# The last norms of a fused two-block model: GpSimd subtracts some means, PSUM operands, and the final norm in two token halves

## The reference

```python
xl = _layernorm(ALPHA * xl + g * out, ln_g, ln_b)       # end of the first block
# second block
h = x * (1.0 + scale) + shift
proj = h @ w_in                                          # q, k, v, g_attn, glu_a, glu_b, g_conv
# ... banded attention; conv of glu_a * sigmoid(glu_b), 31 taps; pointwise product
y = concat([y_attn, y_conv]) @ w_out
x = layer_norm(ALPHA * x + gate * y, ln_g, ln_b)         # mean and variance over the 2048 features
```

## Time and profile before

| what | us |
|---|---|
| median of three runs | 3348.26 (3348.14 to 3349.41) |
| the profiled execution | 3346.11 |
| its span in the profile | 3344.4 |
| PE busy | 3196.6 (96%) |
| DVE busy | 2244.8 (67%) |
| ACT busy | 1324.6 (40%) |
| POOL busy | 265.5 (8%) |

### The profile page before, as it was taken

The page is one execution under the profiler, slowest core; times in us unless marked ns, Lnnn a source line. Parts: engine busy times, 40 slices in busy tenths (PEclk is TensorE's granted clock), DMA queues, the critical chain, the costliest instruction groups (busy, mean ns, idle before and its releaser), DMA issues.

```text
span 3344.4 us, 47678 instructions
## 1 busy us (share of the span) xinstructions
PE 3196.6 (96%) x16612; PEld 2606.6 (78%) x16612; DVE 2244.8 (67%) x3528; ACT 1324.6 (40%) x2023; POOL 265.5 (8%) x490
## 2 busy tenths in 40 slices
PE   5899999999999999999999999999997999999996
PEld 0799989788777777879888777777785877888885
DVE  0677778756777765687656676774677899755446
ACT  0445555323444443237422444443326222455323
POOL 0000011101101100110101000100110000000000
PEclk8899999999999999999999999999998999999998
DMA  9665557555444433654755444432562322222332
GB/s 397 253 226 200 205 191 269 189 214 186 143 153 165 147 114 122 241 192 170 262 187 202 160 139 147 156 116 74 210 215 104 114 101 88 95 90 80 113 114 88
DMA packets 107409, 554.41 MB, mean 166 GB/s; under 512 B 17856, under 2 KB 17904, under 8 KB 64144
## 3 DMA queue, kind: packets, MB, share of 16 engines
q1 hardware_dynamic: 47232, 343.95, 28.8%
q0 software_dynamic: 60048, 208.75, 18.4%
HBM read 530.55 MB, written 22.04 MB: 165 GB/s over the span
## 4 chain that ended last, share of the span: by engine, by line
PE 71%; DVE 9%; DVEq 6%; DMA 5%; issue 5%; ACT 2%; ACTq 1%; POOL 0%; POOLq 0%; SPq 0%
PE acc L1164 21%; PE acc L1166 20%; PE acc L1165 20%; DVEq L2213 4%; DVE w_lo L1589 3%; PE pv L1288 3%; DMA xy<-in_wm 3%; PE S L1262 2%; DMA gates<-in_wm 2%; PE S L1277 1%; DVE gates L1642 1%; DVE xy L2220 1%; PE misc L1299 1%; ACT w_hi L641 1%; DVE xy L2040 1%
## 5 line engine op out<-in xcount | busy, mean ns | idle before, releaser
L1164 PE MATMUL acc<-h_hi,w_hi 128*128 128x512 f32 (+1 forms) x4576 | 1672.5, 365 | 25.4 <-DVE w_lo L1589 14.9
L1166 PE MATMUL acc<-h_hi,w_lo 128*128 128x512 f32 (+1 forms) x4576 | 1641.5, 359 | 0.0
L1165 PE MATMUL acc<-h_lo,w_hi 128*128 128x512 f32 (+1 forms) x4576 | 1640.2, 358 | 0.0
L1164 PEld LDWEIGHTS acc<-h_hi,w_hi 128*128 128x128 f32 x4576 | 865.3, 189 | 182.4 <-issue 37.2
L1165 PEld LDWEIGHTS acc<-h_lo,w_hi 128*128 128x128 f32 x4576 | 866.2, 189 | 128.6 <-issue 6.9
L1166 PEld LDWEIGHTS acc<-h_hi,w_lo 128*128 128x128 f32 x4576 | 865.4, 189 | 129.6
L1589 DVE TENSOR_TENSOR w_lo<-raw,w_hi 128x1024 fp32r<-128x1024 f32 x592 | 698.1, 1220 | 200.7 <-ACT w_hi L641 197.7
L641 ACT ACTIVATE w_hi<-raw 128x1024 fp32r<-128x1024 f32 x592 | 592.9, 1052 | 65.3 <-DMA raw<-in_w 38.5
L641 ACT ACTIVATE ev<-acc 128x512 f32<-128x512 f32 (+1 forms) x210 | 110.7, 531 | 879.0 <-PE acc L1166 857.8
L465 POOL DMA_DIRECT2D gates<-in_wm x288 | 153.6, 533 | 1429.2 <-DVE gates L1642 1237.4
L641 ACT ACTIVATE work<-S,small 128x768 f32<-128x768 f32 (+1 forms) x160 | 129.1, 813 | 257.3 <-DVE small L1756 257.3
(11 more groups left out here) (244 smaller groups left out, 2425.8 us busy)
## 6 DMA issues: line engine op xcount, KB each, us to landing
raw<-in_w SPq DMA_DIRECT2D x296, 1024.0 KB, 4.9
gates<-in_wm POOLq DMA_DIRECT2D x288, 512.0 KB, 4.8
xy<-in_wm SPq DMA_DIRECT2D x32, 1024.0 KB, 8.8
x_d<-xy POOLq DMA_DIRECT2D x2, 4096.0 KB, 14.2
qb<-x_d POOLq DMA_DIRECT2D x16, 256.0 KB, 4.3
kb<-x_d POOLq DMA_DIRECT2D x16, 256.0 KB, 4.2
out_y<-xy POOLq DMA_DIRECT2D x4, 1024.0 KB, 4.2
bias_d<-kb POOLq DMA_DIRECT2D x8, 384.0 KB, 20.7
```

The lines of the kernel that those rows point to most:

```text
L1164: mm(o, w_hi[:, w], h_hi[:, x], start=n == 0, stop=False)
L1165: mm(o, w_hi[:, w], h_lo[:, x], start=False, stop=False)
L1166: last = mm(o, w_lo[:, w], h_hi[:, x], start=False, stop=n == len(ks) - 1)
```

## The change

Four things are changed.

1. Norm "b", statistics. The mean is written to `t1` once, and ACT squares it (`mean_sq`) in place of DVE. Tiles 0 to 3 are lowered by DVE straight from the PSUM sums; tiles 4 to 15 are lowered by POOL (12 `tensor_tensor` of 128x512), ahead of its store in its program. The inverse deviation is written to PSUM (`pv`), and ACT's plain copy of h goes to PSUM (`whole_glu`, two quarters of `S`). The split of the second `glu` weight tile is cut in halves: the first half comes before the last `bout` tile is taken out, DVE's second half after the third pair.
2. `glu` on ACT: each of the three groups of `norm_affine` moves from before the evacuation of tile 0, 1, 2 to behind it.
3. `out2`: the last two weight tiles (14 and 15) run as four products of 256 columns: both tiles for tokens 0 to 255, then both for 256 to 511. The statistics of the first token half are summed on PE inside the third of these; the whole last norm runs once for each token half. Of each half DVE lowers tiles 0 to 7 from PSUM and POOL tiles 8 to 15; DVE multiplies all 16. ACT applies gain and bias to tiles 0 to 10 of the first half and 0 to 11 of the second, POOL to 11 to 15 of the first, DVE to 12 to 15 of the second.
4. The output goes out in six stores from SP: two of the first half (8 tiles each), four of the second (8, 4, 2 and 2 tiles).

```diff
+        whole_glu = (S[:, 2 * SEQ:3 * SEQ], S[:, 3 * SEQ:4 * SEQ])
+        TOKENS = (slice(0, SEQ // 2), slice(SEQ // 2, SEQ))
+        POOL_FIRST, DVE_LAST = 11, 12
+        last_dev = (pv[:, 0:SEQ // 2], misc[:, 0:SEQ // 2])
...
@@ pool @@
             residual("b", "bout", x1_d)
+            pool.wait_ge(rest_ready, shown(rest_ready, 1))
+            for k in range(4, KT):
+                x = tile(xy, k, SEQ)
+                nc.gpsimd.tensor_tensor(x, x, t1[:], ALU.subtract).then_inc(rest_done, 1)
             store("b", x2_d, 48)
...
-            for q in range(4):
-                pool.wait_ge(x_ready, shown(x_ready, 48 + 4 * (q + 1)))
-                pool.dma_start(out[:, 4 * q:4 * (q + 1)], xy3[:, 4 * q:4 * (q + 1)]).then_inc(x_st, 16)
-            pool.wait_ge(x_st, shown(x_st, 48 + 64))
+            for h in range(2):
+                pool.wait_ge(last_rest_ready, shown(last_rest_ready, h + 1))
+                for k in range(8, KT):
+                    x = tile(xy, k, SEQ)[:, TOKENS[h]]
+                    nc.gpsimd.tensor_tensor(x, x, t1[:, TOKENS[h]], ALU.subtract).then_inc(last_rest_done, 1)
+                if h == 0:
+                    for k in range(POOL_FIRST, KT):
+                        ...
+                        nc.gpsimd.tensor_scalar(x, x, vec("ln_g2", k), vec("ln_b2", k), ALU.mult, ALU.add)\
+                            .then_inc(pool_out, 1)
@@ scalar @@
                 if c == "b":
-                    hi(At(TILE0["glu"] + 1))
-                    inverse_deviation("b")
+                    hi(At(TILE0["glu"] + 1), (1,))
+                    act.wait_ge(rest_ready, shown(rest_ready, 1))
+                    f(t2[:], t1[:], ACT.Square).then_inc(mean_sq, 1)
+                    inverse_deviation("b", pv)
...
             def glu(i, first=False):
...
-                    if first and p < 3:
-                        norm_affine("b", SEQ, 1, (0, 6, 11)[p], (6, 11, KT)[p])
                     (the wait for the tile and its evacuation)
+                    if first and p < 3:
+                        norm_affine("b", SEQ, 1, (0, 6, 11)[p], (6, 11, KT)[p])
...
+            for m in range(2):
+                new_square(0, m)
+            last_inverse(0)
+            new_square(1, 0)
+            last_affine(0, 0, POOL_FIRST)
+            new_square(1, 1)
+            last_inverse(1)
+            last_affine(1, 0, DVE_LAST)
@@ tensor @@
+            def last_tiles():
+                for h in range(2):
+                    for m in range(2):
+                        j, a = j_at("out2", 3, 2 + m), a_at("out2", 3, 2 + m)
+                        ... (h == 0: wait for acc_free; h == 1: wait for part_out)
+                        product(acc[a.odd][:, TOKENS[h]], j, range(KT), at=h * SEQ // 2, stride=SEQ, beside_n=6,
+                                beside=(lambda: last_deviation_sums(0)) if (h, m) == (1, 0) else None)\
+                            .then_inc(part_done, 1)
+                last_deviation_sums(1)
@@ vector @@
+                    def variance(h):
+                        cols = TOKENS[h]
+                        dve.wait_ge(stat_done, shown(stat_done, 2 * ST_NO[c] + 2 * h + 1))
+                        ts(t1[:, cols], last_sums[h][0], 1.0 / D, None, ALU.mult)
+                        dve.drain()
+                        dve.sem_inc(last_rest_ready, 1)
+                        ... (square of the mean; variance; then_inc(dev_ready, 1))
+                        for k in range(8):
+                            x = part(c, k)[:, cols]
+                            stt(x, last_sums[h][0], -1.0 / D, x, ALU.mult, ALU.add)
...
+                    evacuated(0, 0)
+                    evacuated(0, 1)
+                    squares(0)
+                    variance(0)
+                    evacuated(1, 0)
+                    scaled_part(0, 0, KT)
+                    evacuated(1, 1)
+                    squares(1)
+                    variance(1)
+                    scaled_part(1, 0, KT)
+                    dve.drain()
+                    for k in range(DVE_LAST, KT):
+                        x = part(c, k)[:, TOKENS[1]]
+                        ts(x, x, vec("ln_g2", k), vec("ln_b2", k), ALU.mult, ALU.add).then_inc(dve_out, 1)
...
-            scaled(0, 2)
-            def next_pair(i, more=True):
-                scaled(i * 2, 2)
-                modulated("g.h", SEQ, i - 1)
-                if more:
-                    less_rest(i * 2 + 2, 2)
-                    dve.drain()
-            loop(dve, 1, KT // 2 - 1, next_pair)
+            scaled(0, 2, pv)
+            def next_pair(i):
+                dve.wait_ge(rest_done, shown(rest_done, At(-2, 2, i)))
+                scaled(i * 2, 2, pv)
+                modulated("g.h", SEQ, i - 1, whole_glu)
+            loop(dve, 1, 4, next_pair)
+            lo(At(TILE0["glu"] + 1), (1,))
+            loop(dve, 4, KT // 2, next_pair)
```

More of the change, by code:

```diff
@@ L451, in _ @@
                 at += i * t
+            x_at = 48
+            for h, first, last, done, n in ((0, 0, 8, x_ready, x_at + 8), (0, 8, KT, pool_out, KT - POOL_FIRST),
+                                            (1, 0, 8, x_ready, x_at + POOL_FIRST + 8),
+                                            (1, 8, DVE_LAST, x_ready, x_at + POOL_FIRST + DVE_LAST),
+                                            (1, DVE_LAST, 14, dve_out, 14 - DVE_LAST),
+                                            (1, 14, KT, dve_out, KT - DVE_LAST)):
+                sp.wait_ge(done, shown(done, n))
+                if done is pool_out:
+                    sp.wait_ge(x_ready, shown(x_ready, x_at + POOL_FIRST))
+                sp.dma_start(out[:, first:last, TOKENS[h]], xy3[:, first:last, TOKENS[h]]).then_inc(out_st, 16)
+            sp.wait_ge(out_st, shown(out_st, 6 * 16))
         @block.gpsimd
@@ L871, in body, with deviation_squares @@
                             modulate_pair("a.h", early_x, SEQ, *by_set(0), n, to=whole_early)
[L873 to L875 removed]
+                def deviation_squares(i, tiles=range(4)):
+                    for p in tiles:
                         j, a, k = j_at(phase, i, p), a_at(phase, i, p), 4 * (i - 2) + p
@@ L907, in inverse_deviation @@
                 act.drain()
-                f(t2[:], t2[:], ACT.Exp, scale=-0.5).then_inc(ln_sd, 1)
+                f(to[:], t2[:], ACT.Exp, scale=-0.5).then_inc(ln_sd, 1)
             def squares_to_add(c, T, g, base=0):
@@ L1143, in _, with new_square, last_inverse, last_affine @@
             project_out("g", "out2", 4)
-            inverse_deviation("g")
-            norm_affine("g", SEQ, 2)
+            hi(At(TILE0["out2"] + KT - 1))
+            for k in (6, 7):
+                act.wait_ge(old_ready, shown(old_ready, 8 * ST_NO["g"] + k + 1))
+                act.wait_ge(ssq_added, shown(ssq_added, 16 * ST_NO["g"] + k + 3))
+                f(ev[(k + 6) % 4][:], tile(xy, k, SEQ), ACT.Square).then_inc(ssq_ready, 1)
+            def new_square(h, m):
+                n = 14 + 2 * h + m
+                act.wait_ge(part_out, shown(part_out, 2 * h + m + 1))
+                act.wait_ge(ssq_added, shown(ssq_added, 16 * ST_NO["g"] + n - 3))
+                f(ev[n % 4][:, TOKENS[h]], tile(xy, 14 + m, SEQ)[:, TOKENS[h]], ACT.Square).then_inc(ssq_ready, 1)
+            def last_inverse(h):
+                act.wait_ge(dev_ready, shown(dev_ready, ST_NO["g"] + h + 1))
+                f(t2[:, TOKENS[h]], t2[:, TOKENS[h]], ACT.Ln, bias=eps[:, 0:1])
+                act.drain()
+                f(last_dev[h], t2[:, TOKENS[h]], ACT.Exp, scale=-0.5).then_inc(ln_sd, 1)
+            def last_affine(h, first, last):
+                for k in range(first, last):
+                    x = tile(xy, k, SEQ)[:, TOKENS[h]]
+                    act.wait_ge(n_ready, shown(n_ready, LN_AT["g"] + KT * h + k + 1))
+                    f(x, x, ACT.Identity, scale=vec("ln_g2", k), bias=vec("ln_b2", k)).then_inc(x_ready, 1)
+            for m in range(2):
[6 more added lines that the diff above has]
+            last_affine(1, 0, DVE_LAST)
         @block.tensor
@@ L1391, in project_out, with body @@
                 T = TOK.get(c, SEQ)
-                def body(i, beside=None, beside_n=3, last=False):
-                    for p in range(4):
+                def body(i, beside=None, beside_n=3, last=False, tiles=range(4)):
+                    for p in tiles:
                         weight_tile(j_at(phase, i, p), a_at(phase, i, p), T, H_AT[c + ".y"], p == 0,
```

124 lines of the change are left out of this document (97 added, 27 removed).

## The result

The changed kernel takes 3332.52 us (median of five runs, 3330.49 to 3333.6); the kernel before, timed with it, 3349.39 (3348.14 to 3352.89). The ratio is 0.9949, 95% interval 0.9938 to 0.996: faster by 0.5%, inside the range, 0.7 us from the predicted 3333.2. The profiled execution took 3333.60 us, with a span of 3332.0.

The account below looks back on a forecast made before the run. PE holds 71% of the span, but glu is paced by DVE, whose run begins when x2's store lands. Gains of 5.1 us at the gated units' start and 10 at the end, 15.1 from 3348.26, give 3333.2 us; range 3325 to 3342.5.

Parts of the forecast that it names:

- A1: Norm b's statistics: first multiplication near 2534.6 instead of 2535.71, gain 1.1 us, from 0 to 1.6.
- A2: Pair loop: period falls from 4.16 to 2.82 us, paced by ACT; first pair of weight tiles ends 8.9 us earlier.
- PSUM operands: Pair loop operands moved to PSUM: no difference taken; 0.06 x 4 us on each pair hidden under ACT.
- The contention: DVE and POOL blocking one another over SBUF inputs: under 2 us added, as most DVE operations have one PSUM input.
- GpSimd: POOL's 12 subtractions in norm b: between 0.62 and 2.35 us each, estimate 1.1, hidden up to about 1.9 each.
- A3: Affines behind evacuations: x2's store leaves 16.1 us after the first pair, lands 5.1 us earlier; new PE wait 5 to 6.
- Part A: Norm b and the start of the gated units: gain 5.1 us, from 0 to 9, kept through glu by DVE.
- B: The kernel's end, out2's last tiles, last norm and stores: gain 9.7, say 10 us, from 4 to 13.
- (1): x2's store lands much sooner, 3 us more, and the DMA tail is 2 us shorter: 20 us, 3328; chance 0.20.
- (2): The end gains half: short operations on DVE's chain, or 1 KB rows, cost 5 us more: 3338; chance 0.16.
- (3): Pair loop stays at 4.16 us and the affines' new order costs 3.8 us: 3341 to 3342; chance 0.10.
- (4): Slower: POOL's subtractions bound norm b and the end, deciding from 2.9 us each; 3360 us at 3.5; chance 0.04.

Follow-up runs that it names:

- the two kernels with groups first: Changed kernel with the third, or all three, groups of norm b's affines back ahead of glu's evacuations: norm b to out2's tile 13 took 759.75 and 759.55 us, against 762.83.
- POOL double: Changed kernel with each of POOL's twelve norm b subtractions done twice: norm b to out2's tile 13 took 774.53 us, against 762.83.
- SBUF operands: Changed kernel with norm b's inverse deviation and modulated-tile buffers back in SBUF: norm b to out2's tile 13 took 771.44 us, against 763.7 at the same clock.
- upper half first: Changed kernel with norm b's affines before evacuations, tiles 8 to 15 first, x2 stored in two DMAs: norm b to out2's tile 13 took 753.51 us.
- combined: Changed kernel plus two x2 stores, tiles 8 to 15 first; POOL lowering ten tiles per last-norm half; second half's first store split: 3324.87 us, ratio 0.9929 to before.

## Why the prediction was right, point by point

**A1**, 1.1 us predicted, 1.27 measured (+13.42 to +12.15) at the same clock. The order was as worked out; that the clock can fall ahead of the sums and cost 0.95 was no term of it, though the bounds of 0 to 1.6 hold it.

**A2.** The period of 2.83 is ACT's four activations, as predicted (2.82). The term that was mis-sized is ACT's run: 24.4 us (2538.03 to 2562.43) where 8 x 2.82 and 1 gave 23.6; ACT waits 1.2 us behind DVE's half weight split, the rest are gaps of 0.2 us between pairs. ACT's end came 8.0 earlier for 8.6. The first pair's end (2567.7, as ACT takes tile 2 out at 2578.73, 0.1 and 10.9 behind it) came 7.9 earlier for 8.9. The clock was back at 1.0 at 2547, 6.5 us after PE's restart at 2540.53, inside the 8 us assumed.

**PSUM operands.** "I take no difference" was right of the operations themselves and wrong as a reading of the edit: they are what keeps POOL's subtractions harmless, and they are worth 7.7 us. The contention that I gave "under 2 us" is small in this kernel only because of them, as the prediction's own clause on inputs in PSUM says; what it did not have is their worth.

**GpSimd.** Taken as hidden, between 0.62 and 2.35: measured 1.24, and DVE never waits for it. The prediction gives the cover twice, as "about 1.9 each" and as 24.6 us (2.05 each); the kernel with the doubled subtractions bears out the second, to 0.3 us.

**A3.** The pattern holds in each piece: the store 15.9 us after the first pair (16.1), landing after 14.06 (14.4), the new wait of PE at tile 5 of 5.5 (5 to 6). (The prediction's "2605.7 - 3" does not give that wait; 2605.7 less the 8.9 us of A2, 2596.8 against 2602.5, does.) Part A is 4.30 for 5.1: the store leaves 4.3 earlier, and the 0.8 lie in A2's end. That the store, not PE, starts `glu` is shown by the two kernels with groups first.

**B**, 10.67 for 9.7 to 10. In the stage's own time (predicted 3301.5 for the first tokens of tile 15, after an evacuation of tile 13 at 3289.42: +12.1) they are out at +12.0 (3299.20 and 0.48); the last DVE affine ends at +38.4 for +38.1, the tail behind it is 5.9 us for 7.2. So the chain's sum was good to 0.3 us. The stores were right as well: from the last affine to the last landing 5.15 us (3326.12 to 3331.27) for 5.1 (3327.5 to 3332.6). The term that was mis-sized stands behind the landing, where the prediction carries 2.1 us over from before and after has 0.76. Before, POOL issues the stores and waits for them, and a drain of POOL of 1.70 us follows its wait. In after SP waits for them, with a drain of 0.08; POOL's own drain ended at 3322.3 and is hidden. The rows of the two drains, of before and of after (their starts are 3342.5 and 3331.7):

```profile
L114 POOLq DRAIN  x1: 1704/1704/1704, 3342.5 to 3342.5; - x1
```

```profile
L114 SPq DRAIN  x1: 77/77/77, 3331.7 to 3331.7; - x1
```

So 1.3 us of B's gain come from the engine that waits for the stores (edit 4), a term that the prediction did not have. The trace shows them; no run moves the wait alone.

**The rivals.** (1) fell: the landing is 14.06, and its 3 us aren't there; the tail is 1.3 us shorter, but by POOL's drain and not by the DMA. (2) fell: the chain as a whole was over by 0.3 us, not by 5. (3) fell: the period is 2.83. (4) as told.

That the median lies 0.7 us from the forecast is partly luck. The stages gave 15.0 for 15.1 because A was forecast 0.8 too high and B 0.7 to 1 too low, the latter for the drain that no term had. The medians differ by 16.9 us, 1.9 more than the stages of the two profiled executions, which is within the scatter of single runs (3330.49 to 3333.6 for after); and before's median in these runs is 1.1 above the one that I started from.

## What to carry to other kernels

Follow a stall to the transfer that ends it. Of 8 us gained ahead of the store, four were lost in the place of the affines, and only a store cut to what the next writer overwrites moved the bound to PE; then a wait that had been free was worth its full length. When GpSimd takes over elementwise work, ask which operands DVE has in SBUF at the same time. Look also at which engine waits for the last transfer and what it still has to do behind it. Where a span scatters by more than the effect, measure from a step ahead of the change to one behind it, at the same granted clock.

## What the runs showed of the hardware

- DVE with two inputs in SBUF beside POOL reading SBUF: 1.75 us for 0.69 (512 columns), POOL 1.53 for 1.24 as the mean of its twelve (SBUF operands). With one of DVE's inputs in PSUM neither changes (after: 0.69 and 1.24). At 256 columns, `t<-t,xy` at 3312.80 took 0.73 for 0.42 beside POOL's affines, 0.3 us on the chain of after. POOL can be the one held up: in POOL double, beside DVE's split of 1024 columns at 2549.28, which kept its 1.22, one subtraction of 1.27 took 2.08:

```profile
2549.57 2.08 POOL L649 TENSOR_TENSOR evt<-xy,t 128x512 f32<-128x512 f32 x1 [0.16 <-issue]
```

- POOL's subtraction takes 1.24 us for 512 columns and 0.69 to 0.73 for 256 (5.51 and 5.82 for eight), twice DVE's 0.62 and 0.34.
- After a wait of PE of 2.1 us the granted clock was at 1.0 in one execution and at 0.5 in another of the same code (after and its repeat); it costs 0.95 us in two short sums. After a wait of 2.5 us it stayed at 1.0 in upper half first and fell to 0.5 in combined, whose code is the same there: tile 2 is taken out 1.6 us later (+58.25 for +56.69).
- Behind its wait for the last stores POOL drains for 1.70 us (before), SP for 0.08 (after).
